# A transformer stack on one Trainium2 core: the modulation projection moves from TensorE to GpSimd

## The chip, the core and the metric

The program runs on one core of one Trainium2 chip. The metric is the device time of one execution in microseconds (us).

## What is computed

The program runs four layers on a sequence of 256 tokens of width 1024 (an attention branch, a residual with factor 8^0.25, a layer norm), and behind them one block with a modulated RMS norm, pooling and MoBA attention, and PEER experts (product keys, 16384 experts in two tables). The kinds of the four attention branches are MLA, sliding window (SWA), forgetting (Fox), MLA, with 16 heads each. All numbers are fp32.

The change concerns the modulation of the last block:

```python
def modulate(x, g, shift, scale):
    return rmsnorm(x, g) * (1 + scale[:, None, :]) + shift[:, None, :]

# w_ada: (1024, 6 * 1024), c: one condition vector of 1024
mod = silu(c) @ w_ada + b_ada      # 6 * 1024 numbers: shift, scale, gate, twice
```

It has one row of output. It depends on nothing that the layers compute, so it can be worked out at any time before the last block's norm.

## The kernel before

**The stream.** All large weights lie in one tensor, `stream`, as chunks of 1 MB (128 rows x 4 tiles x 512 columns) in the order of use. SP loads chunk after chunk into `raw` (2 slots, L411 to L415). A chunk is two pieces of two tiles. For each piece ScalarE writes a rounded high part into `w_hi` (L829), and VectorE the rest, raw minus high, into `w_lo` (L1058); these are rings of 4 pieces. TensorE multiplies high by high, high by low and low by high (`parts_product`, L504 to L506), so that three fp32r products give nearly fp32. Each piece is used once (`piece_used`), which frees its place in the ring. SP waits for `piece_lo` before it fills a slot again.

**The plan.** Every group of products whose sum is taken out of PSUM together is a `Unit` (L130), with its banks, its number of pieces and who takes it out how. Units alternate between two pairs of banks (0 to 3). `bank_free` (L488) waits for the unit before the last. Attention has banks 4 to 7: scores in 4 and 5, turned probabilities in 6, outputs in 7.

**A layer.** TensorE turns x (`xT`), projects it (q, k, v and gates; MLA in two steps with a norm and rotations between), does attention head by head, turns the outputs (`oT`) and projects them with the residual. VectorE's `layer_norm` (L1225) ends the layer. TensorE waits for it, half by half (`x_half`), before it turns x for the next layer.

**Attention** (L564 on TensorE, L873 on ScalarE, L1137 on VectorE). In step i TensorE does the scores of head i (L577; in Fox L581 too), one modulation piece (L552), the turn of head i-1's probabilities (L591) and the output of head i-2 (L601 to L603). VectorE scales and masks the scores (L1165, in SWA L1162), takes their negative maximum (L1169, L1170), and normalises an output by its row sum, times the gate (L1189). ScalarE takes the exponential (L889) and copies the turned probabilities back (L897). These three products are in fp32 without splitting.

**The modulation before.** Each layer has three units of 512 outputs, each of 4 pieces: 12 pieces in 12 of 16 steps (L569 on TensorE). The stationary operand is the condition's column, spread over 128 columns (`c_hi`, `c_lo`), so all 128 rows of the result are alike. ScalarE and VectorE split these pieces inside attention (L898, L1200), VectorE adds the bias to row 0 (L1116), and GpSimd stores the row in `mod_rows` in HBM and loads the next bias (L444 to L450). The weights stand in the stream between a layer's projections and its output weights (`lay_out`, L1572).

**GpSimd's queue before** holds DMA issues alone: start loads, stores and biases, gains of the layer norms (`ln_gb`, needs `ln_used`), and behind the last head (L460) the loads for MoBA: all six modulation rows spread over 128 partitions, gain, pool weights, bands.

**The silu of the condition** is on ScalarE in layer 0, in front of the building of k (L934). VectorE splits it behind the turns (L1312).

MoBA's attention (8 heads) uses the same `attention` with no modulation pieces.

Of the kernel before, what the change touches and what calls it, by code (L numbers as in the profile page):

```python
# [14 lines left out]
F32 = mybir.dt.float32  # L15
# [6 lines left out]
P = 128  # L22
S = 256
B = S // P
D = 1024
# [104 lines left out]
class Unit:  # L130
# [8 lines left out]
    def __init__(self, plan, kind, dst, how, ktiles=KD, cols=COLS, pieces=0, k0=0, col0=0, tiles=4, width=P, pair=None):  # L139
# [4 lines left out]
        self.pair = self.n % PAIRS if pair is None else pair  # L144
        last = plan[-1].count if plan else {"act": 0, "dve": 0}
# [19 lines left out]
def build(nc, x_in, stream, table_in, bands_in, ln_in, mla_norm_in, sinks_in, wf_in, bf_in, c_in, bada_in, g2_in,  # L165
          pool_w_in, pool_scale_in, aug_in, keys_in, x_spill, mod_rows, out):
    n_chunks = stream.shape[0]
    with ExitStack() as ctx:
# [16 lines left out]
        small = sb("small", [P, 64])  # L185

# [12 lines left out]
        c_hi = sb("c_hi", [P, KD], F32R)  # L199
        c_lo = sb("c_lo", [P, KD], F32R)  # L200
# [39 lines left out]
        mod_row = cut(26112, 2, COLS)  # L240
# [50 lines left out]
        def ada_units(l):  # L291

            return [Unit(plan, "own", [mod_row[0:1, n % 2]], [("dve", "add")], pieces=KD // PK)
                    for n in range(ADA_UNITS * l, ADA_UNITS * (l + 1))]

        layers = []
        for l in range(DEPTH):
# [3 lines left out]
            if kind == "mla":  # L301
# [6 lines left out]
                L["ada"] = ada_units(l)  # L308
                L["oT"] = split_turn_units(KD)
            elif kind == "swa":  # L310
# [3 lines left out]
                L["ada"] = ada_units(l)  # L314
                L["oT"] = split_turn_units(KD)
            else:
# [5 lines left out]
                L["ada"] = ada_units(l)  # L322
                L["oT"] = split_turn_units(KD)
            L["out"] = residual_units()
            layers.append(L)
# [45 lines left out]
        bada_loaded = [sem(f"bada_loaded{s}") for s in range(2)]  # L371
        c_silu, c_rep, h_ready, merged_ready = sem("c_silu"), sem("c_rep"), sem("h_ready"), sem("merged_ready")
# [25 lines left out]
        n_pieces = 2 * n_chunks  # L398
# [6 lines left out]
        def _(sp):  # L405
            sp.dma_start(x_tok, x_in.rearrange("(b p) d -> p b d", p=P)).then_inc(x_loaded, 16)
            sp.dma_start(kept[:, :], table_in[:, 0:KEPT_W]).then_inc(kept_loaded, 16)
            for s in range(RAW):
                sp.dma_start(raw[:, s], stream[s]).then_inc(chunk_landed[s], 16)
            sp.dma_start(arena[:, REST:REST + TABLE_W - KEPT_W], table_in[:, KEPT_W:]).then_inc(tables_loaded, 16)  # L410
            with sp.Fori(1, n_chunks // RAW) as turn:  # L411
                for s in range(RAW):

                    sp.wait_ge(piece_lo, 2 * RAW * turn - 2 * RAW + 2 * s + 2)
                    sp.dma_start(raw[:, s], stream[RAW * turn + s]).then_inc(chunk_landed[s], 16)  # L415
# [7 lines left out]
        def _(pool):  # L423
# [5 lines left out]

            load(c_col[:, :], c_in, c_loaded)  # L430
# [6 lines left out]
            def load_bias(n):  # L437
                load(mod_row[0:1, n % 2], bada_in[:, n * COLS:(n + 1) * COLS], bada_loaded[n % 2])

            for n in range(2):  # L440
                load_bias(n)
# [18 lines left out]
            pool.wait_ge(out_taken, DEPTH * HEADS)  # L460
            load(moba["mod"].rearrange("p a n -> p (a n)"), rows(mod_rows[0]), mod_loaded)
            load(gain, rows(g2_in[0]), g2_loaded)
            load(moba["pw"], pool_w_in, moba_loaded)
            load(moba["ps"], pool_scale_in, moba_loaded)

            pool.wait_ge(ln_used, DEPTH)
            load(moba["bands"].rearrange("p a b n -> p (a b n)"), bands_in, moba_loaded)

# [16 lines left out]
        def _(pe):  # L485
            piece = [0]

            def bank_free(unit):  # L488
                if unit.n >= PAIRS and unit.pair < PAIRS:
                    wait_put(pe, [plan[unit.n - PAIRS]])  # L490
# [61 lines left out]
            def ada_piece(units, i):  # L552

                u, first = units[i // (KD // PK)], i % (KD // PK) * PK
                if first == 0:
                    pe.wait_ge(c_rep, 1)
                    bank_free(u)
                w = take_piece()
                for k in range(first, first + PK):
                    mm = parts_product(bank_of(u, 0), [c[:, k:k + 1].broadcast_to([P, P]) for c in (c_hi, c_lo)],  # L560
                                       [x[:, k % PK] for x in w], k == 0, k == KD - 1)
                drop_piece(mm)

            def attention(heads, q, k, v, fox=False, ada=()):  # L564
# [54 lines left out]
            for L in layers:  # L619
# [7 lines left out]
                if L["kind"] == "mla":  # L627
# [12 lines left out]
                    for u in L["kT"]:  # L640
# [3 lines left out]
                              lambda h, b: mla["kv"][:, b, 2 * HD * h + HD:2 * HD * (h + 1)], ada=L["ada"])  # L644
                    o = mla["o"]
                elif L["kind"] == "swa":
# [4 lines left out]
                    def half(h):  # L651
# [5 lines left out]
                              lambda h, b: attn["v"][:, b, HD * (h // SWA_GROUP):HD * (h // SWA_GROUP + 1)], ada=L["ada"])  # L657
                    o = attn["o"]
                else:
# [10 lines left out]
                    for u in L["k"] + L["v"] + L["gate"]:  # L670
# [4 lines left out]
                              lambda h, b: attn["v"][:, b, HD * h:HD * (h + 1)], fox=True, ada=L["ada"])  # L675
# [139 lines left out]
        def _(act):  # L815
# [57 lines left out]
            def attention(heads, kind, ada=()):  # L873
                g0 = heads_done[0]
                before = ada[0].pieces_done - KD // PK if ada else 0
                for i in range(heads + 1):
# [21 lines left out]
                    if 1 <= i <= len(ada) * KD // PK:  # L898

                        split_ahead(before + i)  # L900
# [739 lines left out]
```

## Time and profile before

| | |
|---|---|
| median of 3 runs | 1908.87 us (1907.85 to 1910.93) |
| profiled execution, device time | 1908.54 us |
| its span | 1906.3 us |
| mean granted TensorE clock | 0.93 of full speed |
| TensorE busy | 1733.4 us, 91% |
| VectorE busy | 1285.2 us, 67% |
| ScalarE busy | 905.6 us, 48% |
| GpSimd busy | 23.8 us, 1% |
| HBM traffic | 283 MB, mean 148 GB/s |

Names in the profile: PE is TensorE's matmuls, PEld its weight loads, DVE VectorE, ACT ScalarE, POOL GpSimd. L504 is a line of the kernel above; a helper's line stands for all its callers. "Busy" of PE comes from modelled ends of pipelined products, so a busy PE isn't one at its peak. The granted clock is a share of 2.4 GHz: 0.50 is 1.2 GHz, and values between are the mean of a stretch that has both. Groups have the form: line, engine, operation, output<-inputs, shape, count | busy us, mean ns | idle time before them in us and who ended it. Most SBUF tensors are cuts of one tensor, `arena`.

### The profile page before, as it was taken

Reading aid. Unit: us, or ns where it says so; the run is one execution under the profiler, and the core shown is the slowest. Engines: PE = TensorE matmul, PEld = TensorE weight load, DVE = VectorE, ACT = ScalarE, POOL = GpSimd, SP = SyncE. Lnnn points to the kernel's source line nnn. Section 1 sums busy time; section 2 is a strip of 40 time slices with the busy share of each in tenths; the row PEclk is TensorE's granted clock in tenths of the full one; section 3 lists DMA queues with packets and bytes.
Section 4 is the critical chain, followed back from the end, with each engine's and each line's share of the span. In section 5 each row is a group of like instructions: output and inputs, shape, how many; then the busy total and the mean of one; then the engine's idle time right before and its main releaser. Section 6 shows DMA issues by size and latency. Waiting matters only on the chain.

```text
span 1906.3 us, 29464 instructions
## 1 busy us (share of the span) xinstructions
PE 1733.4 (91%) x10294; PEld 1534.0 (80%) x10294; DVE 1285.2 (67%) x2391; ACT 905.6 (48%) x1410; POOL 23.8 (1%) x50
## 2 busy tenths in 40 slices
PE   6788898898989787898879999899999999999996
PEld 5677787796867576686769999899999888888885
DVE  3666557544756685544555999777777888885554
ACT  4464355344543573343334666655555333334543
POOL 0000000000000000000000000000000000000000
PEclk8888897899988897896889999999999999999998
DMA  6423443355234434451343444433433343435552
GB/s 225 175 90 110 160 162 126 110 177 177 92 108 164 174 111 171 166 182 62 113 152 135 174 176 176 177 132 132 146 140 134 130 154 132 154 138 215 198 188 99
DMA packets 40323, 282.95 MB, mean 148 GB/s; under 512 B 5280, under 2 KB 5424, under 8 KB 6848
## 3 DMA queue, kind: packets, MB, share of 16 engines
q1 hardware_dynamic: 37136, 267.13, 39.7%
q0 software_dynamic: 3120, 14.94, 2.2%
q8 instruction: 40, 0.66, 0.1%
q14 instruction: 27, 0.22, 0.0%
HBM read 279.94 MB, written 2.12 MB: 148 GB/s over the span
## 4 chain that ended last, share of the span: by engine, by line
PE 73%; DVE 17%; ACT 4%; DMA 3%; issue 3%; DVEq 0%; SPq 0%; ACTq 0%
PE banks L504 20%; PE banks L506 19%; PE banks L505 19%; PE banks L771 6%; DVE w_lo L1058 5%; DMA raw<-stream 3%; PE banks L577 2%; PE banks L546 2%; PE banks L591 1%; ACT w_hi L829 1%; PE banks L603 1%; PE banks L602 1%; PE banks L601 1%; DVE arena L1440 1%; DVE arena L1247 1%
## 5 line engine op out<-in xcount | busy, mean ns | idle before, releaser
L1058 DVE TENSOR_TENSOR w_lo<-raw,w_hi 128x1024 fp32r<-128x1024 f32 x504 | 614.2, 1221 | 385.8 <-ACT w_hi L829 383.9
L829 ACT ACTIVATE w_hi<-raw 128x1024 fp32r<-128x1024 f32 x504 | 532.2, 1057 | 635.8 <-PE banks L506 549.1
L504 PE MATMUL banks<-w_hi,xT_hi 128*128 128x512 f32 (+2 forms) x1140 | 457.0, 401 | 25.9 <-DVE xT_lo L1090 15.4
L506 PE MATMUL banks<-w_hi,xT_lo 128*128 128x512 f32 (+2 forms) x1140 | 448.5, 393 | 0.0
L505 PE MATMUL banks<-w_lo,xT_hi 128*128 128x512 f32 (+2 forms) x1140 | 446.8, 392 | 0.0
L504 PE MATMUL banks<-xT_hi,w_hi 128*128 128x256 f32 x1360 | 394.8, 290 | 5.5 <-DVE w_lo L1058 2.6
L506 PE MATMUL banks<-xT_hi,w_lo 128*128 128x256 f32 x1360 | 388.8, 286 | 0.0
L505 PE MATMUL banks<-xT_lo,w_hi 128*128 128x256 f32 x1360 | 388.7, 286 | 0.0
L504 PEld LDWEIGHTS banks<-w_hi,xT_hi 128*128 128x128 f32 x1140 | 220.5, 193 | 72.7 <-issue 17.5
L504 PEld LDWEIGHTS banks<-xT_hi,w_hi 128*128 128x128 f32 x1360 | 265.0, 195 | 7.4 <-ACT arena L988 2.7
L505 PEld LDWEIGHTS banks<-xT_lo,w_hi 128*128 128x128 f32 x1360 | 264.7, 195 | 0.0
L506 PEld LDWEIGHTS banks<-xT_hi,w_lo 128*128 128x128 f32 x1360 | 264.3, 194 | 0.0
L506 PEld LDWEIGHTS banks<-w_hi,xT_lo 128*128 128x128 f32 x1140 | 219.1, 192 | 46.2
L505 PEld LDWEIGHTS banks<-w_lo,xT_hi 128*128 128x128 f32 x1140 | 220.7, 194 | 42.5
L546 PE MATMUL banks<-kept,arena 128*128 128x128 f32 (+1 forms) x354 | 69.8, 371 | 92.4 <-DVEq L1267 29.1
L546 PEld LDWEIGHTS banks<-kept,arena 128*128 128x128 f32 (+1 forms) x354 | 58.8, 189 | 101.5 <-DVEq L1267 30.8
L771 PEld LDWEIGHTS banks<-scratch 128*128 128x128 f32 x1024 | 129.9, 192 | 5.3
L771 PE MATMUL banks<-scratch 128*128 128x64 f32 x1024 | 128.2, 268 | 0.0
L889 ACT ACTIVATE scratch<-scratch,neg_max 128x128 f32<-128x128 f32 (+1 forms) x144 | 64.0, 445 | 75.1 <-DVE neg_max L1170 74.6
L1495 DVE TENSOR_TENSOR arena<-arena,banks 128x256 f32 (+1 forms) x128 | 53.7, 420 | 52.0 <-PE banks L771 52.0
L1485 DVE TENSOR_TENSOR scratch<-kept,scratch 128x512 f32<-128x512 f32 x128 | 87.6, 684 | 0.3 <-ACT scratch L869 0.3
L869 ACT ACTIVATE arena<-banks 128x512 f32<-128x512 f32 (+1 forms) x76 | 43.6, 587 | 85.0 <-PE banks L506 65.1
(178 smaller groups left out, 1589.8 us busy)
## 6 DMA issues: line engine op xcount, KB each, us to landing
raw<-stream SPq DMA_DIRECT2D x252, 1024.0 KB, 4.8
arena<-ln_in POOLq DMA_DIRECT2D x4, 1024.0 KB, 5.1
arena<-mod_rows POOLq DMA_DIRECT2D x1, 3072.0 KB, 10.1
arena<-g_in POOLq DMA_DIRECT2D x3, 512.0 KB, 9.6
arena<-x_in SPq DMA_DIRECT2D x1, 1024.0 KB, 5.1
arena<-bands_in POOLq DMA_DIRECT2D x1, 1024.0 KB, 5.2
arena<-keys_in POOLq DMA_DIRECT2D x1, 1024.0 KB, 5.2
x_spill<-arena POOLq DMA_DIRECT2D x1, 1024.0 KB, 5.0
```

The source lines that it names most:

```text
L504: pe.matmul(out, stationary[0], moving[0], start=first, stop=False, **k)
L505: pe.matmul(out, stationary[0], moving[1], start=False, stop=False, **k)
L506: return pe.matmul(out, stationary[1], moving[0], start=False, stop=last, **k)
L546: mm = pe.transpose(bank_of(unit, t // 2)[0:unit.width, (t % 2) * S + b * P:(t % 2) * S + (b + 1) * P], src[:, b, c:c + unit.width], ident)
L577: mm = pe.matmul(bank[:, cols[0]:cols[1]], qh[:, qb * P:(qb + 1) * P], kh[:, 0:n], start=(qb == 0), stop=not fox, skip_group_check=True)
L771: mm = pe.matmul(banks[:, 4 + s % 2, t * HALF:(t + 1) * HALF], hot2[:, s % 2, t], hot1[:, s % 2, t], start=(t == 0), stop=True, skip_group ...
L829: act.activation(w_hi[:, s], raw[:, s // 2, (s % 2) * PIECE:(s % 2 + 1) * PIECE], ACT.Copy).then_inc(piece_hi, 1)
L869: act.activation(dst, src, fn).then_inc(evac_act, 1)
L889: ins = act.activation(probs[:, g % 2, lo:hi], s_sb[:, g % 2, lo:hi], ACT.Exp, bias=neg_max[:, g % 4, b:b + 1], accum_out=row_sum[:, g % 4 ...
L1058: dve.tensor_tensor(w_lo[:, s], raw[:, s // 2, (s % 2) * PIECE:(s % 2 + 1) * PIECE], w_hi[:, s].bitcast(F32), ALU.subtract).then_inc(piece ...
L1485: dve.tensor_tensor(hot2[:, s % 2], keys.broadcast_to([P, GT, NKEYS]), picks[1].broadcast_to([P, GT, NKEYS]), ALU.is_equal)
L1495: dve.tensor_tensor(mine, mine, banks[:, 4 + s % 2, 0:GT * HALF].rearrange("p (t n) -> p n t", t=GT), ALU.mult).then_inc(g_taken, 1)
```

## The change

The modulation leaves the stream. GpSimd loads the weights tile by tile (128 rows x 512 columns, 256 KB), two slots (`ada_raw`), multiplies a tile by the condition's column (one number per partition) and adds it to one of three sums (`ada_sum`, 128 x 512), which start as zero with the bias in row 0. When a layer's 24 tiles are in, TensorE sums over the partitions: one product with ones per 512 outputs, in plain fp32, behind the layer's out projection, into banks 4 to 6. ScalarE copies row 0 of each back over the sum's row 0 and GpSimd stores it.

Attention has no modulation piece any more. SP's loop over the stream is written out for the layers, without their 24 modulation chunks (`n_pieces` is 456, not 504), and is a loop again behind them. The silu of the condition is ScalarE's first work. The modulation rows are loaded for the last block in two halves, the first behind layer 3's last head, the second when all are stored.

```diff
@@ plan
-        def ada_units(l):
-
-            return [Unit(plan, "own", [mod_row[0:1, n % 2]], [("dve", "add")], pieces=KD // PK)
-                    for n in range(ADA_UNITS * l, ADA_UNITS * (l + 1))]
+        def ada_units():
+
+            return [Unit(plan, "own", [t[0:1] for t in ada_sum[0:2]], [("act", "copy")] * 2, pair=2),
+                    Unit(plan, "own", [ada_sum[2][0:1]], [("act", "copy")], pair=3)]
...
             L["out"] = residual_units()
+            L["ada"] = ada_units()
@@ GpSimd
+            def load_tile(t):
+                k = t % CK
+                load(ada_raw[:, t % 2], stream[tile_chunk[t]][:, k * COLS:(k + 1) * COLS], tile_landed[t % 2])
...
+            for t in range(2):
+                load_tile(t)
+            pool.wait_ge(c_silu, 1)
             for l in range(DEPTH):
 
-                for i, u in enumerate(layers[l]["ada"]):
-                    n = ADA_UNITS * l + i
-                    wait_put(pool, [u])
-                    pool.dma_start(mod_rows[:, n * COLS:(n + 1) * COLS], mod_row[0:1, n % 2]).then_inc(mod_stored, 16)
-                    pool.wait_ge(mod_stored, 16 * (n + 1))
-                    if n + 2 < ADA_UNITS * DEPTH:
-                        load_bias(n + 2)
+                for i in range(ADA_UNITS):
+                    n = ADA_UNITS * l + i
+                    if l:
+                        pool.wait_ge(mod_stored, 16 * ADA_UNITS * l)
+                    pool.memset(ada_sum[i], 0.0).then_inc(sum_cleared, 1)
+                    pool.wait_ge(sum_cleared, n + 1)
+                    load(ada_sum[i][0:1], bada_in[:, n * COLS:(n + 1) * COLS], bada_loaded)
+                pool.wait_ge(bada_loaded, 16 * ADA_UNITS * (l + 1))
+                for i in range(ADA_UNITS):
+                    for k in range(KD):
+                        t = (ADA_UNITS * l + i) * KD + k
+                        pool.wait_ge(tile_landed[t % 2], 16 * (t // 2 + 1))
+                        pool.tensor_scalar(ada_raw[:, t % 2], ada_raw[:, t % 2], c_col[:, k:k + 1], None, ALU.mult).then_inc(tile_scaled, 1)
+                        pool.wait_ge(tile_scaled, t + 1)
+                        pool.tensor_tensor(ada_sum[i], ada_raw[:, t % 2], ada_sum[i], ALU.add).then_inc(ada_used, 1)
+                        pool.wait_ge(ada_used, t + 1)
+                        if t + 2 < DEPTH * ADA_UNITS * KD:
+                            load_tile(t + 2)
+                if l == DEPTH - 1:
+                    pool.wait_ge(out_taken, DEPTH * HEADS)
+                    load(moba["mod"][:, 0:3].rearrange("p a n -> p (a n)"), rows(mod_rows[0, 0:3 * D]), mod_loaded)
+                    load(gain, rows(g2_in[0]), g2_loaded)
...
+                for i in range(ADA_UNITS):
+                    n = ADA_UNITS * l + i
+                    wait_put(pool, [layers[l]["ada"][i // 2]])
+                    pool.dma_start(mod_rows[:, n * COLS:(n + 1) * COLS], ada_sum[i][0:1]).then_inc(mod_stored, 16)
@@ TensorE
-            def ada_piece(units, i):
...
+            def ada_rows(l):
+
+                pe.wait_ge(ada_used, ADA_UNITS * KD * (l + 1))
+                pe.wait_ge(out_taken, heads_done[0])
+                for i in range(ADA_UNITS):
+                    mm = pe.matmul(banks[:, 4 + i], const("ones")[:, 0:P], ada_sum[i], start=True, stop=True)
+                    if i:
+                        mm.then_inc(unit_full, 1)
...
                 for i in range(heads + 2):
                     if i < heads:
                         scores(i)
-                    if i < len(ada) * KD // PK:
-                        ada_piece(ada, i)
...
                 for i, u in enumerate(L["out"]):
                     project(u, L["oT"][1:] if i == 0 else ())
+                ada_rows(l)
@@ ScalarE
-                    if 1 <= i <= len(ada) * KD // PK:
-
-                        split_ahead(before + i)
...
             act.wait_ge(eps_ready, 1)
+            act.wait_ge(c_loaded, 16)
+            act.activation(c_col[:, :], c_col[:, :], ACT.Silu).then_inc(c_silu, 1)
...
                 deviation(root, 1.0, 4, mean_var[:, :, 1])
+                for u in L["ada"]:
+                    evacuate_only(u)
@@ VectorE
-                    if 2 <= i <= len(ada) * KD // PK + 1:
-                        split_ahead(before + i - 1)
-                        if (i - 1) % (KD // PK) == 0:
-                            evacuate_only(ada[(i - 1) // (KD // PK) - 1])
```

## Rows read from the trace of the kernel before

**Rows 1.** Page, parts head and 2: span, and clock granted in 40 slices.
```profile
span 1906.3 us, 29464 instructions
...
PEclk8888897899988897896889999999999999999998
```

**Rows 2.** Page, part 4: the chain that ended last, by line.
```profile
PE banks L504 20%; PE banks L506 19%; PE banks L505 19%; PE banks L771 6%; DVE w_lo L1058 5%; DMA raw<-stream 3%; PE banks L577 2%; PE banks L546 2%; PE banks L591 1%; ACT w_hi L829 1%; PE banks L603 1%; PE banks L602 1%; PE banks L601 1%; DVE arena L1440 1%; DVE arena L1247 1%
```

**Rows 3.** Groups by line and form, TensorE: one of three modulation groups.
```profile
L504 PE MATMUL banks<-w_hi,c_hi 128*128 128x512 f32 x96 | 45.3, 472 | 0.0
```

**Rows 4.** Busy by window, four attentions; last columns clock, DMA share, GB/s.
```profile
118.26:161.45 43.19, 39.71 (x249) 34.03 (x248) 38.84 (x99) 31.78 (x85) 2.42 (x5) 1.00 0.38 128
271.65:321.33 49.68, 46.02 (x243) 35.75 (x242) 44.22 (x128) 34.27 (x102) 2.44 (x5) 0.92 0.42 143
474.09:533.92 59.83, 58.62 (x313) 46.76 (x314) 43.71 (x113) 31.38 (x86) 2.44 (x5) 0.93 0.31 106
673.16:717.24 44.08, 40.08 (x243) 34.08 (x242) 38.88 (x99) 32.80 (x87) 1.96 (x4) 0.95 0.39 135
```

**Rows 5.** Busy by window, layer attention without modulation pieces beside it.
```profile
471.00:477.00 6.00, 5.85 (x15) 4.00 (x16) 1.78 (x6) 0.98 (x4) 0.00 (x0) 0.50 0.27 112
529.40:541.00 11.60, 10.05 (x41) 8.60 (x39) 4.75 (x18) 3.21 (x11) 0.97 (x2) 0.50 0.26 91
713.20:725.00 11.80, 9.11 (x38) 7.97 (x39) 5.77 (x20) 3.63 (x13) 0.48 (x1) 0.50 0.26 91
```

**Rows 6.** Busy by window, MoBA attention: six steps, then one step.
```profile
882.01:903.58 21.57, 20.42 (x73) 15.60 (x74) 9.74 (x35) 9.13 (x34) 0.00 (x0) 0.50 0.00 1
889.26:892.84 3.58, 3.58 (x14) 2.81 (x15) 1.72 (x7) 1.36 (x5) 0.00 (x0) 0.50 0.00 0
```

**Rows 7.** Timeline, layer 0 attention: start us, us, engine line, [idle before].
```profile
119.65 0.56 DVE L1165 SCALAR_TENSOR_TENSOR scratch<-banks,arena 128x384 f32<-128x384 f32 x1 [0.18 <-PE banks L577]
...
161.45 0.55 DVE L1165 SCALAR_TENSOR_TENSOR scratch<-banks,arena 128x384 f32<-128x384 f32 x1
...
164.18 0.87 PE L591 MATMUL banks<-kept,scratch 128*128 128x128 f32 x3 [0.55 <-ACT scratch L897]
```

**Rows 8.** Timeline, TensorE: ends of attention in layers 3 and 2.
```profile
708.10 0.52 PE L591 MATMUL banks<-kept,scratch 128*128 128x128 f32 x3 [0.98 <-ACT scratch L897]
...
709.08 0.87 PE L577 MATMUL banks<-arena 96*128 96x128 f32 x4
...
713.77 0.88 PE L591 MATMUL banks<-kept,scratch 128*128 128x128 f32 x3 [0.99 <-ACT scratch L897]
...
717.18 0.87 PE L591 MATMUL banks<-kept,scratch 128*128 128x128 f32 x3
...
528.99 0.87 PE L591 MATMUL banks<-kept,scratch 128*128 128x128 f32 x3 [0.44 <-ACT scratch L897]
...
533.82 0.90 PE L591 MATMUL banks<-kept,scratch 128*128 128x128 f32 x3
```

**Rows 9.** Groups by line and form, VectorE: two inputs in SBUF.
```profile
L1265 DVE TENSOR_TENSOR arena<-arena 128x512 f32<-128x512 f32 x8 | 5.2, 687 | 0.1
```

**Rows 10.** DMA issues: a load of 256 KB by GpSimd, us to landing.
```profile
arena<-aug_in POOLq DMA_DIRECT2D x1, 256.0 KB, 5.7
```

**Rows 11.** Timeline, GpSimd, when layer 0 ends.
```profile
207.14 0.56 POOL L425 DMA_DIRECT2D arena<-ln_in  x1 [42.08 <-DVEq L1252]
```

**Rows 12.** Timeline, TensorE: last product of layer 1.
```profile
357.21 0.39 PE L506 MATMUL banks<-w_hi,xT_lo 128*128 128x512 f32 x1
```

**Rows 13.** Groups by line and form, VectorE, 207 to 271 us.
```profile
L1058 DVE TENSOR_TENSOR w_lo<-raw,w_hi 128x1024 fp32r<-128x1024 f32 x21 | 25.7, 1225 | 32.9 <-ACT w_hi L829 32.7
```

**Rows 14.** Start: busy by window, and ScalarE's timeline.
```profile
10.00:16.00 6.00, 0.39 (x3) 0.15 (x2) 1.60 (x2) 3.55 (x4) 0.00 (x0) 0.79 1.01 402
...
15.73 1.06 ACT L829 ACTIVATE w_hi<-raw 128x1024 fp32r<-128x1024 f32 x1 [0.42 <-DMA raw<-stream]
```

**Rows 15.** Timeline, TensorE, layer norm of layer 0.
```profile
203.76 1.97 PE L546 MATMUL banks<-kept,arena 128*128 128x128 f32 x8 [6.52 <-DVEq L1250]
```

More of the change, by code:

```diff
@@ L144, in __init__ @@
         self.pair = self.n % PAIRS if pair is None else pair
+        same = [u for u in plan if u.pair == self.pair]
+        self.before = same[-1] if same else None
         last = plan[-1].count if plan else {"act": 0, "dve": 0}
@@ L321, in build @@
                 L["gate"] = token_units(attn["gate"], D, SILU2)
-                L["ada"] = ada_units(l)
                 L["oT"] = split_turn_units(KD)
+            L["chunks"] = (plan[-1].pieces_done - (layers[-1]["out"][-1].pieces_done if layers else 0)) // 2
             L["out"] = residual_units()
+            L["ada"] = ada_units()
             layers.append(L)
@@ L407, in _ @@
             sp.dma_start(kept[:, :], table_in[:, 0:KEPT_W]).then_inc(kept_loaded, 16)
[L408 to L411, printed above, removed]
+            landed, at = 0, 0
+            for L in layers:
+                n_in, n_out = L["chunks"], 2 * D // COLS
+                for n in list(range(at, at + n_in)) + list(range(at + n_in + ADA_CHUNKS, at + n_in + ADA_CHUNKS + n_out)):
+                    if landed >= RAW:
+                        sp.wait_ge(piece_lo, 2 * (landed - RAW) + 2)
+                    sp.dma_start(raw[:, landed % RAW], stream[n]).then_inc(chunk_landed[landed % RAW], 16)
+                    landed += 1
+                    if landed == RAW:
+                        sp.dma_start(arena[:, REST:REST + TABLE_W - KEPT_W], table_in[:, KEPT_W:]).then_inc(tables_loaded, 16)
+                at += n_in + ADA_CHUNKS + n_out
+            with sp.Fori(at // RAW, n_chunks // RAW) as turn:
                 for s in range(RAW):
-                    sp.wait_ge(piece_lo, 2 * RAW * turn - 2 * RAW + 2 * s + 2)
+                    sp.wait_ge(piece_lo, 2 * RAW * turn - 2 * RAW + 2 * s + 2 - 2 * DEPTH * ADA_CHUNKS)
                     sp.dma_start(raw[:, s], stream[RAW * turn + s]).then_inc(chunk_landed[s], 16)
@@ L428, in rows @@
                 return src.partition_broadcast(P)
+            tile_chunk, at = [], 0
+            for L in layers:
+                at += L["chunks"]
+                tile_chunk += [at + n // CK for n in range(ADA_UNITS * KD)]
+                at += ADA_CHUNKS + 2 * D // COLS
+            def load_tile(t):
+                k = t % CK
+                load(ada_raw[:, t % 2], stream[tile_chunk[t]][:, k * COLS:(k + 1) * COLS], tile_landed[t % 2])
             load(c_col[:, :], c_in, c_loaded)
@@ L458, in _ @@
                     load(mla["g"], rows(mla_norm_in[1]), norm_loaded)
[L460 to L464, printed above, removed]
             pool.wait_ge(ln_used, DEPTH)
             load(moba["bands"].rearrange("p a b n -> p (a b n)"), bands_in, moba_loaded)
+            pool.wait_ge(mod_stored, 16 * DEPTH * ADA_UNITS)
+            load(moba["mod"][:, 3:6].rearrange("p a n -> p (a n)"), rows(mod_rows[0, 3 * D:]), mod_loaded)
             pool.wait_ge(h_ready, 1)
@@ L488, in bank_free @@
             def bank_free(unit):
-                if unit.n >= PAIRS and unit.pair < PAIRS:
-                    wait_put(pe, [plan[unit.n - PAIRS]])
+                if unit.before is not None and unit.pair < PAIRS:
+                    wait_put(pe, [unit.before])
             def take_piece():
@@ L550, in _, with attention @@
             heads_done = [0]
-            def ada_piece(units, i):
[L554 to L564, printed above, removed]
+            def ada_rows(l):
[5 more added lines that the diff above has]
+                        mm.then_inc(unit_full, 1)
+            def attention(heads, q, k, v, fox=False):
                 g0 = heads_done[0]
@@ L871, in _, with attention @@
             heads_done = [0]
-            def attention(heads, kind, ada=()):
+            def attention(heads, kind):
                 g0 = heads_done[0]
-                before = ada[0].pieces_done - KD // PK if ada else 0
                 for i in range(heads + 1):
@@ L1133, in _, with attention @@
             heads_done = [0]
-            biases = [0]
             gated = s_sb[:, :, :].rearrange("p a n -> p (a n)")[:, 0:COLS].unsqueeze(1)
-            def attention(heads, kind, scale, o, gate, ada=()):
+            def attention(heads, kind, scale, o, gate):
                 g0 = heads_done[0]
-                before = ada[0].pieces_done - KD // PK if ada else 0
                 def head_rows(h):
@@ L1323, in _ @@
                     wait_put(dve, L["gate"])
-                    attention(HEADS, "swa", HD ** -0.5, attn["o"], attn["gate"], L["ada"])
+                    attention(HEADS, "swa", HD ** -0.5, attn["o"], attn["gate"])
                 else:
@@ L1346, in _ @@
                     settle()
-                    attention(HEADS, "fox", HD ** -0.5, attn["o"], attn["gate"], L["ada"])
+                    attention(HEADS, "fox", HD ** -0.5, attn["o"], attn["gate"])
                 for u in L["oT"]:
```

43 lines of the change are left out of this document (16 added, 27 removed).

## The prediction

> **What bounds the kernel now.** I read the page first. The profiled execution lasts 1906.3 us inside a run of 1908.54 us (2.2 us lie around the span), and that run is 0.3 us below the median of the three runs, 1908.87; every sum below starts from 1908.54. The tenths of the granted clock in the page's second part are mostly 8 and 9 in the first half and 9 behind it [rows 1]: TensorE doesn't always have its full clock. The fourth part, the chain that ended last, is mostly TensorE, and of that mostly projections [rows 2]. GpSimd computes nothing, so it is free.
>
> The 48 modulation pieces (288 products: the group shown and two like it [rows 3]) all stand in the first 12 of 16 heads of the four layers' attention. So the change has to be read in four stretches. I cut them from the first to the last score pass of VectorE (L1165 or L1162), 15 steps from head to head: 43.19, 49.68, 59.83 and 44.08 us, together 196.8 us [rows 4]. The granted clock is 1.00 (2.4 GHz) over the first one and 0.92 to 0.95 over the others, and the reader is to see why: where the pieces have ended it is 0.50 (1.2 GHz) [rows 5]. The fifth attention of the kernel, MoBA's, has no such pieces. There the clock is 0.50 from end to end, with TensorE occupied for 20.4 of 21.6 us, and a head takes 3.58 us [rows 6]. It is a picture of what attention looks like when modulation has left it.
>
> **Part 1: the pieces leave the heads.** Gone are 12 times 6 products per layer on TensorE, 12 splits each on ScalarE and VectorE, and three adds on VectorE. What a head costs without them depends on the clock.
>
> At 2.4 GHz: from VectorE's score pass (161.45) to the turn of the probabilities on TensorE (164.18) are 2.73 us [rows 7]; from the start of a turn (708.10) through the head's outputs to the end of the next scores (709.08 + 0.87) are 1.85 us [rows 8]. Scores run one head ahead, so this loop of 2.73 + 1.85 + 0.1 serves two heads: 2.34 us a head. It is less than the 2.9 us of today (43.19 / 15), so work does leave the path, since today VectorE's split of 1.22 us stands in each head.
>
> At 1.2 GHz: an MLA head goes from turn to turn in 717.18 - 713.77 = 3.41 us with no wait in front [rows 8], a MoBA head in 3.58 us [rows 6], and a forgetting head, which has two more products, in 533.82 - 528.99 = 4.83 us [rows 8]. TensorE then is the bound by its own slowness, and ScalarE and VectorE, now relieved, only wait.
>
> I take 1.2 GHz, because every attention of the trace shows it as soon as nothing but head work is left: in both tails of [rows 5], and in MoBA [rows 6], where TensorE never waits and yet the clock doesn't rise. The products with the modulation weights are dense 512-column work that fills the gaps between heads, so they hold the clock; the change removes just these. The Trainium skill says the same as a rule (TensorE: Matmul & The Clock Gate, "The HAM clock gate"): the slow clock is the default and only activity releases it. By it this change costs; by TensorE's removed work alone it would gain; the trace agrees with the rule.
>
> Stretch by stretch, with a few steps at full clock after a warm projection:
> - MLA, layers 0 and 3: the first step as now, 1.4 (118.26 to 119.65 [rows 4, 7]), one of 2.3, then 13 of 3.41: 48.0 us against 43.19 and 44.08: +4.8 and +3.9.
> - Sliding window: 1.4, two of 2.6 (2.34 and the sink's small operations), 12 of 3.58: 49.6 against 49.68: -0.1.
> - Forgetting: its attention begins cold already (0.50 from 471 to 477 [rows 5]), so a first step of 2.9, one of 3.5 (no outputs yet) and 13 of 4.83: 69.2 against 59.83: +9.4.
>
> Sum of part 1: +18.0 us. What follows attention starts at 1.2 GHz before and after, so it doesn't change. If the clock holds one step longer in each stretch, that takes off 1.1 us in each.
>
> **Part 2: GpSimd's work.** Per layer it issues three clears, three bias loads and 24 tiles: a load of 256 KB, a product, a sum. No row shows GpSimd computing. The nearest is VectorE's 128x512 with both inputs in SBUF, 0.69 us [rows 9]; for lack of a nearer row I bound one operation by 0.69 and by three times that. A load of that size took 5.7 us to land [rows 10], and an issue takes 0.56 us of GpSimd [rows 11]. With two buffers a tile takes the larger of its own work (two operations and an issue, 1.9 to 4.7 us) and half of load plus own work (3.8 to 5.2 us): 3.8 to 5.2 us, 91 to 125 us a layer. The sliding layer leaves least time, from 207.1 us [rows 11] to the end of its out projection at 357.6 us [rows 12], 6.0 us a tile after the bias loads. So it is hidden. A page only prices the sum: the Trainium skill (GPSIMD Engine Reference, "Elementwise") has 4.5 us for 2048 elements, an estimate of 1.1 us for 512.
>
> Queued behind the 24 tiles on GpSimd's queue are the stores of the modulation rows, the next norm's gains (needed a whole layer later) and, in layer 3, the loads for MoBA, which even before could only start behind the last head. None is late at that pace.
>
> **Contention.** The splits before attention read two SBUF tensors, and VectorE sat idle 32.9 us in front of 21 of them, 1.6 us each [rows 13]; a delay by a GpSimd operation goes into that. On the path are only some norm and rotation operations. Bounds 0 (all in idle time) and 66 us (each of 96 tiles delays the path once by 0.69 us); I take 2 us, near the lower end, since splits have that cover.
>
> **Part 3: start.** From 10 to 16 us the DMA engines are full, 402 GB/s, and ScalarE waits for the second chunk until 15.73 us [rows 14]. Two tiles more, 0.5 MB, at that rate: +1.3 us (0 if they come last). The silu of the condition moves from the path of layer 0 to the start, but its table is then loaded in front of the gates' silu: nothing.
>
> **Part 4: ada_rows.** TensorE waits for the last tile, then does three fp32 products of 512 columns behind the out projection. A head's scores, 384 columns in fp32, take 0.87 us at full clock [rows 8], so three times 512 columns cost 3.5 us (7 at half the clock, but the projection leaves it full), and TensorE is idle there for 6.52 us for the layer norm [rows 15]. ScalarE's three copies of a row lie in front of its first evacuation. Nothing; if that cover went, up to 3.5 us a layer. SP's loads in attention vanish (24 chunks), and nobody waited for them.
>
> **Sum:** 1908.5 + 18.0 + 2 + 1.3 = 1929.8, say 1930 us.
>
> **The rivals.**
> 1. **The clock stays at 2.4 GHz** (the other side). For it: the heads then come closer together than in today's tails, where VectorE still splits. Stretches: 34.2 twice, 36.4 with the sink's operations, and for the forgetting heads 15 of 2.65 (half of 4.83 - 3.58 at full clock, over two heads), 39.8: 144.6 against 196.8, so 1908.5 - 52.2 + 3.3 = 1860 us. Against it: four tails and MoBA. It decides from about a third of the way: the cold sum is 214.8, and 193.5 breaks even.
> 2. **Only the forgetting layer gets the full clock**, since its heads have the most TensorE work: 2.9 + 3.5 + 13 times 2.65 = 40.9 against 59.83, -19, so 1908.5 + 8.6 - 19 + 3.3 = 1901 us. For it: no row shows a longer run of such heads without pieces. Against: its own tail fell to 0.50 too [rows 5].
> 3. **VectorE is held up by GpSimd.** If GpSimd's operations push VectorE's back wherever both run, a third of the 66 us above may reach the path in place of 2: 1950 us. For it: both read SBUF at once in the projections; against: the idle time of [rows 13]. The Trainium skill (SBUF — State Buffer, "Who interferes with whom") says that a VectorE instruction with two SBUF inputs and a GpSimd instruction that reads SBUF exclude each other; no row of before, where GpSimd doesn't compute, can show it.
> 4. **GpSimd is late**, and TensorE waits in ada_rows. It decides at 6.0 us a tile in the sliding layer and at 7.0 in layer 3; at 8 us it is 48 + 24 us more, 2002 us. Against: the upper bound is 5.2.
>
> **Chances.** Forecast 0.66 (own range 1920 to 1942); rivals 0.08, 0.14, 0.08, 0.04. About 0.2% (3.8 us) is what a measurement of this kernel can tell. Faster by more: rival 1 and most of rival 2, 0.19; within: the rest of it, 0.07; slower 0.74. The range goes from 1899 (rival 2) to 1945 us.
>
> **What would show it.** In the changed profile: granted clock 0.50 over most of each attention and MLA heads 3.4 us apart, forgetting heads 4.8; VectorE and ScalarE less busy there; a GpSimd that finishes its 24 tiles before the heads end; three products in the idle time of the layer norm. Heads of 2.3 us at clock 1.00 would prove me wrong, and so would TensorE waiting for GpSimd's sums, or VectorE's splits clearly above 1.22 us and on the chain.

## The result, and the profile after

The changed kernel takes 1938.0 us (median of 4 runs, 1936.1 to 1947.2) against 1908.5 us before, measured beside it. The ratio is 1.0162, 95% interval 1.0127 to 1.0196: slower by 29.5 us. Forecast were 1930 us and a range from 1899 to 1945.

The profiled execution lasts 1936.13 us, its span is 1934.3 us. First the page after: span, busy time by engine, granted clock.

```profile
span 1934.3 us, 28816 instructions
PE 1749.2 (90%) x10030; PEld 1541.6 (80%) x10030; DVE 1271.8 (66%) x2329; ACT 865.4 (45%) x1374; POOL 398.9 (21%) x351
...
PEclk8776885899558788897779999999999999999998
```

TensorE has 264 products fewer and is busy 16 us longer. GpSimd is at work for 399 us (24 before). The clock has new dips where attention is ([rows 1] has none at 5).

Next the four layer attentions by window, cut as in [rows 4], from first to last score pass. Columns: stretch, length, busy time (and instructions) of PE, PEld, DVE, ACT and POOL, clock, DMA share, GB/s.

```profile
124.68:170.82 46.14, 43.82 (x178) 39.18 (x179) 24.58 (x85) 21.29 (x75) 2.98 (x3) 0.52 0.04 12
279.43:333.72 54.29, 49.45 (x177) 38.11 (x178) 37.64 (x113) 22.80 (x89) 41.13 (x36) 0.51 0.25 83
488.65:557.91 69.26, 67.96 (x236) 53.64 (x235) 28.82 (x99) 20.00 (x74) 3.15 (x3) 0.50 0.03 8
711.34:746.04 34.70, 26.74 (x176) 21.59 (x176) 24.58 (x85) 21.12 (x75) 1.53 (x2) 0.91 0.00 1
```

Three of four are at about 1.2 GHz (0.50 to 0.52) and longer than before, by 3.0, 4.6 and 9.4 us. The fourth, layer 3's, is at 0.91 and 9.4 us shorter. Together they take 204.4 us against 196.8: +7.6 us. I call everything else in the span "the rest": 1934.3 - 204.4 = 1729.9 us, against 1709.5 before, +20.4 us. So most of the loss lies outside attention, in stretches whose TensorE work the change doesn't touch. The worst are those from the latent norm to the end of q's rotation in the two MLA layers. Here they are after, layers 0 and 3:

```profile
50.34:101.04 50.70, 37.95 (x158) 31.50 (x156) 37.06 (x50) 20.49 (x26) 44.66 (x35) 0.78 0.60 213
635.36:687.33 51.97, 38.29 (x164) 31.48 (x162) 37.39 (x49) 20.71 (x26) 46.82 (x38) 0.80 0.62 221
```

And before, the same two stretches:

```profile
49.51:91.83 42.32, 33.09 (x158) 26.81 (x156) 27.98 (x50) 20.73 (x26) 0.00 (x0) 0.88 0.52 182
608.57:649.78 41.21, 32.74 (x164) 26.96 (x162) 28.07 (x49) 20.84 (x26) 0.00 (x0) 0.92 0.54 199
```

+8.4 and +10.8 us, with the same 50 and 49 instructions on VectorE, which are busy 9 us longer. (TensorE's clock is lower there too. That it isn't the cause shows below: e8 has 0.80 in layer 0's stretch and takes 42.95 us.) The timeline of VectorE and GpSimd in layer 3's rotation shows why (start us, us, engine line):

```profile
680.06 1.38 POOL L477 TENSOR_TENSOR arena<-arena 128x512 f32<-128x512 f32 x1
680.20 1.52 DVE L1227 TENSOR_TENSOR arena<-arena 128x256 f32<-128x256 f32 x1
681.64 0.41 DVE L1228 TENSOR_TENSOR arena<-arena 128x256 f32<-128x256 f32 x1
...
684.24 1.26 POOL L477 TENSOR_TENSOR ada_spare<-arena,ada_spare 128x512 f32<-128x512 f32 x1
684.26 1.51 DVE L1228 TENSOR_TENSOR arena<-arena 128x256 f32<-128x256 f32 x1
```

An operation of 0.41 us that starts during GpSimd's sum lasts 1.5 us: it ends 0.28 us after GpSimd's does. GpSimd's own groups over the whole span (the third sum lies in `ada_spare`):

```profile
L475 POOL TENSOR_SCALAR arena<-arena,c_col 128x512 f32<-128x512 f32 x96 | 172.9, 1801 | 33.1 <-DMA ada_spare<-bada_in 25.5 <-DMA arena<-stream 3.6
L477 POOL TENSOR_TENSOR arena<-arena 128x512 f32<-128x512 f32 x64 | 96.2, 1503 | 5.3
L477 POOL TENSOR_TENSOR ada_spare<-arena,ada_spare 128x512 f32<-128x512 f32 x32 | 42.3, 1320 | 2.7
```

GpSimd's operations are stretched as well: the shortest product took 1.56 us and the shortest sum 1.26 us, where the means are 1.80 and 1.50.

### The profile page after: what moved, and what is told of

It reads as the page before. It is cut to its first block, busy times and chain, and to the rows that moved or that the text cites. A ratio compares the mean times of both kernels' runs of the same rounds, so it can differ in the third digit from the quotient of the medians.

```text
span 1934.3 us, 28816 instructions
## 1 busy us (share of the span) xinstructions
PE 1749.2 (90%) x10030; PEld 1541.6 (80%) x10030; DVE 1271.8 (66%) x2329; ACT 865.4 (45%) x1374; POOL 398.9 (21%) x351
## 4 chain that ended last, share of the span: by engine, by line
PE 71%; DVE 16%; ACT 5%; DMA 4%; issue 3%; DVEq 0%; SPq 0%; ACTq 0%
PE banks L541 18%; PE banks L543 17%; PE banks L542 17%; PE banks L804 6%; DMA raw<-stream 4%; DVE w_lo L1088 4%; PE banks L611 4%; PE banks L625 2%; PE banks L583 2%; ACT w_hi L862 1%; PE banks L637 1%; PE banks L636 1%; PE banks L615 1%; PE banks L635 1%; ACT scratch L921 1%
## 5 line engine op out<-in xcount | busy, mean ns | idle before, releaser
L1088 DVE TENSOR_TENSOR w_lo<-raw,w_hi 128x1024 fp32r<-128x1024 f32 x456 | 577.4, 1269 | 378.9 <-ACT w_hi L862 376.9
L862 ACT ACTIVATE w_hi<-raw 128x1024 fp32r<-128x1024 f32 x456 | 482.0, 1058 | 663.0 <-PE banks L543 532.1
L543 PEld LDWEIGHTS banks<-w_hi,xT_lo 128*128 128x128 f32 x1140 | 223.1, 196 | 46.8
L475 POOL TENSOR_SCALAR arena<-arena,c_col 128x512 f32<-128x512 f32 x96 | 172.9, 1801 | 33.1 <-DMA ada_spare<-bada_in 25.5
L611 PE MATMUL banks<-arena 64*128 64x128 f32 (+3 forms) x288 | 103.1, 502 | 12.7 <-DVE arena L1170 10.2
```

The costliest lines, as they stand in the source:

```text
L475: pool.tensor_scalar(ada_raw[:, t % 2], ada_raw[:, t % 2], c_col[:, k:k + 1], None, ALU.mult).then_inc(tile_scaled, 1)
L543: return pe.matmul(out, stationary[1], moving[0], start=False, stop=last, **k)
L611: mm = pe.matmul(bank[:, cols[0]:cols[1]], qh[:, qb * P:(qb + 1) * P], kh[:, 0:n], start=(qb == 0), stop=not fox, skip_group_check=True)
L862: act.activation(w_hi[:, s], raw[:, s // 2, (s % 2) * PIECE:(s % 2 + 1) * PIECE], ACT.Copy).then_inc(piece_hi, 1)
L1088: dve.tensor_tensor(w_lo[:, s], raw[:, s // 2, (s % 2) * PIECE:(s % 2 + 1) * PIECE], w_hi[:, s].bitcast(F32), ALU.subtract).then_inc(piece ...
```

## The experiments

Stretches are cut in each profile as above. "Attentions" is the sum of the four layers' windows, "rest" is the span less that. The ratio is taken over the executions of a run, and isn't quite the quotient of two medians. "Hold n" stands for n added products a step in the sliding window, forgetting and MoBA attentions; MLA attention has two in e4, e5, e6 and e9, and four in e7.

| | median us | ratio to before | span | attentions | rest |
|---|---|---|---|---|---|
| before | 1908.5 | | 1906.3 | 196.8 | 1709.5 |
| changed | 1938.0 | 1.0162 | 1934.3 | 204.4 | 1729.9 |
| e1 no tiles | 1923.5 | 1.0071 | 1906.9 | 201.9 | 1705.0 |
| e2 loads, writes only | 1922.5 | unclear | 1914.1 | 202.5 | 1711.6 |
| e3 products and sums only | 1935.6 | 1.0168 | 1922.2 | 203.0 | 1719.2 |
| e4 hold 2 | 1957.8 | 1.0250 | 1954.5 | 220.0 | 1734.5 |
| e5 hold 4 | 1894.1 | 0.9916 | 1896.7 | 176.4 | 1720.3 |
| e6 hold 6 | 1908.3 | 1.0003 | 1910.2 | 181.8 | 1728.4 |
| e7 before, hold 4 | 1888.6 | 0.9898 | 1883.3 | 193.9 | 1689.4 |
| e8 pause | 1935.4 | 1.0135 | 1934.9 | 214.2 | 1720.7 |
| e9 hold 4 and pause | 1879.3 | 0.9840 | 1882.6 | 175.2 | 1707.4 |

e2's four times scatter too far for a ratio (1895.9 to 2254.9 us); only its profile is used.

Span, attentions and rest are those of one profiled execution, which can lie far from the median: e1's took 1908.7 us (median 1923.5), e3's 1924.1 us (median 1935.6, the others 1935.0 to 1950.5). How much one stretch varies can be read off before the first score pass, up to which the changed kernel, e4, e5 and e6 have the same program: they reach it at 124.7, 127.6, 128.4 and 124.8 us; the kernel before and e7 at 118.3 and 115.2. A difference of 3 to 4 us in one stretch of one profile shows nothing by itself.

### Which part of GpSimd's work costs: e1, e2, e3

e1:

```diff
-            for t in range(2):
-                load_tile(t)
...
-                for i in range(ADA_UNITS):
-                    for k in range(KD):
...
-                pe.wait_ge(ada_used, ADA_UNITS * KD * (l + 1))
+                pe.wait_ge(bada_loaded, 16 * ADA_UNITS * (l + 1))
```

> Edit: the changed kernel without its 96 tile loads, products and sums (left out: the product with the modulation weights; the sums hold only the bias). Everything else, ada_rows too, stays. In the changed kernel's profile the four layer attentions together take 204.4 us (196.8 before) and all the rest is 20.4 us longer than before. Theory: attention is slow by the clock alone and the rest by GpSimd's work, so here the rest falls back to the 1709.5 us of before (within 3) while attention stays at 1.2 GHz, about 200 to 218 us: time about 1912 to 1930 us. Rival (the rest comes from the order of the stream or from ada_rows): the rest stays 15 us or more above before and the time near 1936.

e2, in place of product and sum (TensorE waits for the biases here too):

```diff
+                        for j in range(6):
+                            pool.memset(ada_raw[:, t % 2], 0.0).then_inc(ada_used, 1)
+                            pool.wait_ge(ada_used, 6 * t + j + 1)
```

> Edit: the changed kernel with all 96 tile loads, but in place of product and sum six clears of the tile per tile, so that GpSimd is about as busy and loads at about the same pace, yet only writes SBUF (left out: the product with the modulation weights). If GpSimd's reads hold VectorE: VectorE's two-input operations keep 1.22 us per split, and the time is that of the kernel without tiles plus at most 4 us for the loads. If the loads (or GpSimd's activity as such) cost the 20 us: the time stays within 5 us of the changed kernel.

e3 drops `load_tile` and the waits for it:

> Edit: the changed kernel with products and sums over two tiles cleared once, and no tile loads (left out: the real weights). If GpSimd's reads hold VectorE: most of the 20 us outside attention stays (15 us or more over the kernel without tiles). If the loads do it: within 4 us of the kernel without tiles.

Without tiles the rest is 1705.0 us, 4.5 less than before (forecast was within 3): no cost of ada_rows or of the new order of the stream is to be seen. The operations of VectorE, in layer 3's projections, with writes only (e2):

```profile
L1087 DVE TENSOR_TENSOR w_lo<-raw,w_hi 128x1024 fp32r<-128x1024 f32 x27 | 32.8, 1223 | 28.1 <-ACT w_hi L861 27.7
L1230 DVE TENSOR_TENSOR arena<-arena 128x256 f32<-128x256 f32 x2 | 0.8, 424 | 0.1
```

and with products and sums but no loads (e3; the second line is the same operation of the rotation, and of its six the one that was held most):

```profile
L1085 DVE TENSOR_TENSOR w_lo<-raw,w_hi 128x1024 fp32r<-128x1024 f32 x27 | 39.2, 1465 | 26.9 <-ACT w_hi L859 26.6
L1228 DVE TENSOR_TENSOR arena<-arena 128x256 f32<-128x256 f32 x2 | 2.9, 1448 | 0.1
```

In e2 GpSimd is busy for about as long (387 us) and loads all tiles, and these two-input operations of VectorE keep their times of before (1.22 and 0.42 us). In e3 it loads nothing, and they are stretched as in the changed kernel, whose splits take 1.45 us there. VectorE's 2329 instructions are busy for 1227.1 us in e1, 1231.7 in e2, 1263.9 in e3 and 1271.8 in the changed kernel. And the two stretches from the latent norm to the rotation show it directly. With writes only (e2):

```profile
50.30:93.93 43.63, 33.02 (x158) 26.77 (x156) 27.96 (x50) 20.50 (x26) 36.10 (x69) 0.88 0.66 238
626.75:667.83 41.08, 32.84 (x164) 27.05 (x162) 28.03 (x50) 20.85 (x26) 35.12 (x68) 0.92 0.70 256
```

and with products and sums but no loads (e3):

```profile
49.11:100.42 51.31, 37.46 (x158) 31.46 (x156) 39.38 (x50) 20.73 (x26) 48.85 (x28) 0.81 0.43 152
624.73:675.37 50.64, 38.38 (x164) 32.00 (x162) 38.23 (x49) 20.84 (x26) 48.09 (x29) 0.82 0.45 163
```

e1 has 40.6 and 41.6 us for them, about as long as before. So VectorE's operations with two inputs in SBUF are held up by GpSimd instructions that read SBUF, not by GpSimd being busy with writes, and not by its DMA. That is what the Trainium skill states (SBUF — State Buffer, "Who interferes with whom").

In the rest, e3 stands 14.2 us over e1, just under the 15 expected. e2 stands 6.6 us over e1, more than the 4 expected, but it is 5.9 us later at the first score pass, 3.3 us longer in the stretch behind it and 4.0 us shorter behind layer 2's attention, so whether loads cost anything isn't shown. Both together (the changed kernel) stand at +24.9.

e1 shows a second thing, the two MLA attentions, layers 0 and 3:

```profile
114.03:148.76 34.73, 26.77 (x176) 21.61 (x176) 24.56 (x85) 21.14 (x75) 0.00 (x0) 0.91 0.00 1
672.79:718.93 46.14, 43.82 (x178) 39.19 (x179) 24.55 (x85) 21.32 (x75) 0.00 (x0) 0.50 0.00 1
```

Same code, same kernel: one at full clock, one at half, 11.4 us apart, and the other way round than in the changed kernel. An MLA attention without pieces can go either way. e1's ten times fall into two groups: three lie at 1908.4 to 1909.2, seven at 1922.4 to 1928.6. The profiled execution is of the lower group and has one slow MLA attention; a second one would add 11.4 us, and the groups are 13 to 20 apart, so this may be part of the difference but not all of it, and no slower execution has a trace. The changed kernel's spread (1936 to 1947) would fit it too, and isn't shown either. Forgetting attention took 69.3 us and was at 0.50 in every changed kernel without added products.

### Is it the clock: e4, e5, e6, e7

These add products that nobody reads, behind each step's scores, with n per step (`hold`). The edit has one thing more, which isn't printed here: in front of the heads TensorE waits for the next piece's split, and behind the first scores for the gate's sums to be taken out of PSUM (sliding window and forgetting), since the added products read the one and write over the other.

```diff
+                    if i < heads + 1:
+                        for _ in range(hold):
+                            pe.matmul(banks[:, 0], w_hi[:, piece[0] % RING, 0:P], w_hi[:, piece[0] % RING, 0:COLS], start=True, stop=True)
```

> Edit: the changed kernel with two idle-time products (128 x 512, fp32r, w_hi by w_hi into bank 0, whose result nobody reads) in each step of all five attentions, behind the scores. Clock theory: if these 0.47 us a step keep 2.4 GHz, MLA heads come 2.4 to 2.6 us apart, forgetting heads 2.7 to 3.1, MoBA heads 2.4 to 2.6, the five attentions take 160 to 185 us in place of 227, and the time falls by 40 to 60 us below the changed kernel, to 1875 to 1900, below the kernel before. If two are too few: clock 0.5 and each cold step 0.85 us longer, 1990 us. Rival (heads are slow for another reason than the clock, the chain through ScalarE and VectorE): the steps grow or stay as they are, whatever the clock.

> Edit: the changed kernel with idle-time products as in e4, two a step in MLA attention, but four in the sliding window, forgetting and MoBA attentions. With two a step these three stayed at 0.50 (64.3, 84.3, 28.8 us). Clock theory: what counts is how dense the work is; if four are enough the clock is above 0.9 there and TensorE's own steps are 1.85 + 0.94 = 2.8 us, forgetting 3.4: 42 to 44, 51 to 53 and 20 to 21 us, time 1895 to 1910. If four are still too few, each cold step grows by another 0.85 us: 77, 97, 35 us and 1985 us. Rival (the clock has nothing to do with the extra products): clock 0.50 whatever their number.

> Edit: as e5, with six a step in the sliding window, forgetting and MoBA attentions, which is the product count of a modulation piece. Clock theory: clock above 0.9 there as in the kernel before, steps of about 3.27 us (forgetting 3.9), so 49, 58 and 23 us, and the time 1912 to 1925: the 20 us that GpSimd's work costs outside attention stay. Rival: the clock stays at 0.50 and the time goes above 2000 us.

e7 has them in the kernel before the change, in steps without a modulation piece:

> Edit: the kernel before the change, its modulation pieces in place, with four idle-time products in each step that has no piece: the last steps of the four layer attentions and all of MoBA's. Clock theory: MoBA's 22.7 us fall to about 20 and the tails gain 1 to 3 us each, with the turns and the first products behind them at full clock: 5 to 20 us faster than before, 1888 to 1903, and faster than both kernels. If the clock isn't held: 10 to 25 us slower.

Sliding window, forgetting and MoBA attention with two products a step (e4):

```profile
272.31:336.65 64.34, 61.54 (x203) 46.67 (x203) 33.92 (x114) 22.81 (x89) 37.71 (x33) 0.51 0.19 66
491.74:576.05 84.31, 84.31 (x271) 65.03 (x271) 29.35 (x98) 20.02 (x74) 4.09 (x4) 0.50 0.02 7
922.17:950.97 28.80, 28.80 (x91) 20.87 (x91) 10.93 (x37) 9.14 (x34) 0.00 (x0) 0.50 0.00 1
```

and with four (e5):

```profile
274.23:319.93 45.70, 43.83 (x233) 33.56 (x234) 34.19 (x114) 22.80 (x90) 36.19 (x32) 0.93 0.26 87
470.88:528.91 58.03, 58.03 (x301) 45.57 (x302) 29.14 (x99) 20.24 (x74) 10.02 (x9) 0.89 0.06 19
876.59:898.44 21.85, 21.85 (x105) 16.10 (x106) 10.94 (x37) 9.25 (x34) 0.00 (x0) 0.85 0.00 0
```

With twice as many added products these attentions take 18.6, 26.3 and 7.0 us less. TensorE has more to do, and nothing was taken from ScalarE or VectorE; what fell is the time of TensorE's own products, with the clock at 0.85 to 0.93 in place of 0.5. So the clock theory stands and the rival (the chain through ScalarE and VectorE) falls. e4's own forecast failed: two products were too few for these three, and its 1957.8 us lie between the 1875 to 1900 of one case and the 1990 of the other, since MLA attention did hold its clock. e5's time (1894.1) lies just below its 1895 to 1910, but its attentions are longer than forecast, 58.0 us for forgetting where 51 to 53 stood: a step took 3.57 us, not 3.4, and the first three took 4.9, 5.5 and 4.8. MLA attention, 35.0 to 36.4 us, was at 0.91 to 0.95 in all of e4, e5, e6 and e9, eight times of eight. With six products, as many as a modulation piece had, the clock is 1.00 and 0.97 in sliding window and forgetting attention, 48.4 and 60.7 us, 2.7 and 2.6 us more than with four. In all, e6 is as fast as the kernel before: 1.0003 (0.9987 to 1.0020), a little under its 1912 to 1925, and its rest of 1728.4 us still has what GpSimd costs. That it comes out even is no measure of what the change lost by the clock, since the products speed up stretches that were at 0.50 before the change as well, as e7 shows.

e7 is within its forecast, 0.9898 (0.9879 to 0.9916). Its four attentions gain only 2.9 us, MoBA's 1.0. Of the 20 us by which the rest is shorter, 16 lie behind the five attentions, where work follows a tail that now ends at full clock. Here are the 4.0 us of layer 0, from its last score pass to the turning of x, in e7 and in the kernel before:

```profile
158.32:196.66 38.34, 28.33 (x142) 23.15 (x140) 22.11 (x39) 14.88 (x24) 0.49 (x1) 0.96 0.30 105
161.45:203.76 42.31, 32.25 (x137) 26.85 (x137) 22.19 (x39) 14.98 (x24) 0.48 (x1) 0.81 0.26 95
```

The other 3.1 us lie before the first score pass, where e7 changes nothing.

### Keeping GpSimd off the path: e8, e9

```diff
+                        if l % 3 == 0 and KD * i + k == 7:
+                            pool.wait_ge(q_roped, l // 3 + 1)
```

> Edit: the changed kernel, but in the two MLA layers GpSimd does seven tiles and then waits until the rotation of q has ended before the other 17. In the changed kernel the stretch from the latent norm to the end of the rotation lasts 50.7 us (layer 0) and 52.0 us (layer 3), against 42.3 and 41.2 before. Theory (GpSimd's reads hold VectorE on the path there): the stretch falls back to 41 to 44 us in both layers, the time by 12 to 19 us, to 1919 to 1928, give or take the 11.4 us by which one MLA attention differs between its two clocks. Rival (the delay comes from elsewhere): the stretch stays near 50 us, the time within 5 us of the changed kernel. If GpSimd then ends too late, TensorE waits in ada_rows and the rest grows instead.

> Edit: e5 (four idle-time products a step, two in MLA) with the pause of e8. If the two costs are independent they add: e5's 1894.1 less 12 to 19 us, 1875 to 1882 us, below the 1888.6 of the kernel before with idle-time products. If holding the clock had already hidden GpSimd's interference, the pause gives less than 5 us more.

The two norm-to-rotation stretches with the pause (e8):

```profile
50.74:93.69 42.95, 36.31 (x158) 30.30 (x156) 29.50 (x50) 20.72 (x26) 4.16 (x4) 0.80 0.54 194
628.90:674.76 45.86, 37.69 (x164) 31.47 (x162) 32.61 (x49) 20.84 (x26) 9.37 (x8) 0.81 0.54 197
```

Layer 0's falls from 50.7 to 43.0 us, as forecast. Layer 3's falls from 52.0 to 45.9, two short of it: there GpSimd still does eight operations in the stretch (POOL, 9.37 us). The rest is 9.2 us shorter than in the changed kernel. The time missed its forecast, 1935.4 us where 1919 to 1928 stood. In the profile both MLA attentions are at 0.50 (46.14 us each), where the changed kernel had one at 0.91: 11.4 us lost by that, near the 9.2 won. The forecast had named this difference; that e8's three other executions had it too isn't shown. With the clock held, where no such chance is left, the pause shows its worth: e9's two stretches take 43.1 and 46.8 us (e5 52.2 and 50.2), and e9 takes 1879.3 us, 14.8 less than e5, within its forecast. At 0.9840 (0.9823 to 0.9856) it is faster than both kernels and than e7.

## Why the prediction was right in direction, and where its sum was off

**The loop and the slow heads** were right in size. The prediction had 3.41 us for a slow MLA head, 3.58 for a sliding one, 4.83 for a forgetting one, 2.34 at full clock. VectorE's score passes are 3.20 us apart in layer 0, 3.58 to 3.86 in layer 1, 4.86 in layer 2, and alternate between 2.2 and 2.4 in layer 3. Forgetting attention was forecast to the digit (69.2, measured 69.26), partly by luck: its first two steps took 1.4 and 4.7 us where 2.9 and 3.5 stood. MLA in layer 0 came to 46.14 for a forecast of 48.0. The row that I took 3.41 from (the turn at 717.18 in [rows 8]) wasn't free of pieces. VectorE still had the last split and the bias add in front of that head's score pass, and the turn follows such a pass by 2.7 us, as in [rows 7]; a step without them takes 3.20. VectorE in the kernel before:

```profile
712.73 1.22 DVE L1058 TENSOR_TENSOR w_lo<-raw,w_hi 128x1024 fp32r<-128x1024 f32 x1
713.86 0.67 DVE L1116 TENSOR_TENSOR arena<-banks,arena 1x512 f32<-1x512 f32 x1
714.46 0.53 DVE L1165 SCALAR_TENSOR_TENSOR scratch<-banks,arena 128x384 f32<-128x384 f32 x1
```

**The sliding window** came to 54.3 for a forecast of 49.6. The two steps at full clock that the forecast had weren't there (e1, without tiles: 3.87 and 3.58 us for them, 51.8 in all), and GpSimd adds the rest. From its seventh score pass (299.26) to the last but one (330.14) every step takes 3.86 us. VectorE's sink operation, two numbers a row and 0.23 us by itself, is held as well, as the timeline of VectorE and GpSimd in the changed kernel shows:

```profile
308.02 1.27 POOL L477 TENSOR_TENSOR ada_spare<-arena,ada_spare 128x512 f32<-128x512 f32 x1
308.22 1.10 DVE L1196 TENSOR_SCALAR neg_max<-neg_max,neg_sink 128x2 f32<-128x2 f32 x1
```

This operation is held by clears too, which only write. In e2 it took up to 0.90 us, and here 0.54, beside three clears in a row:

```profile
285.80 1.69 POOL L476 MEMSET arena<- 128x512 f32 x3
286.39 0.54 DVE L1195 TENSOR_SCALAR neg_max<-neg_max,neg_sink 128x2 f32<-128x2 f32 x1
```

So what e2 shows of writes holds for the two-input operations, not for every operation of VectorE.

**Layer 3's attention** is the term of part 1 that failed. "I take 1.2 GHz" was wrong for it in this execution; rival 1 was right there, and with 34.70 us its price (34.2) was too. The forecast took one clock for all four, and no rival had the two MLA layers differ. e1 shows that for MLA it is open, and the difference is 11.4 us each. Part 1 was forecast at +18.0 and is +7.6 in this profile.

**Contention** is the other term. I took 2 us "near the lower end, since splits have that cover". The cover argument holds where it was made, in the long projections of layers 1 and 2: the stretch up to layer 1's attention is 1.6 us shorter than before, that up to layer 2's 2.2 us longer, neither more than a stretch varies by itself. Yet the splits did come out longer, one of the signs that the prediction had named against itself: 1.45 us in layer 3's projections, not 1.22. The argument doesn't hold in MLA's norm, short projections and rotation, where two-input operations of VectorE follow one another on the path: +8.4 and +10.8 us. These two stretches are 19.2 us of the rest's +20.4. Rival 3, with 22 us for contention in place of 2, describes them. So the forecast's 1930 was near 1938 partly because two errors of opposite sign met: 10 us too much for attention, 17 too little beside it.

**GpSimd's pace** was right: 4.2 to 4.4 us a tile in a layer's mean (forecast 3.8 to 5.2), and its tiles landed in 3.2 us (bounded by 5.7). An operation took 1.3 to 1.8 us in the mean of its group, twice to nearly three times VectorE's 0.69; TensorE never waited for its sums. Rival 4 is out.

**ada_rows** is hidden, as said, and cheaper than the 3.5 us estimated. In layer 0 it runs from 204.62 to 207.36, before x is turned:

```profile
204.62 1.88 PE L594 MATMUL banks<-arena 128*128 128x512 f32 x4
...
206.34 1.02 PE L594 MATMUL banks<-ada_spare,arena 128*128 128x512 f32 x2
...
211.28 1.23 PE L583 MATMUL banks<-kept,arena 128*128 128x128 f32 x8 [3.93 <-DVEq L1269]
```

**The start** is 0.9 us later (first projection at 20.46 us, before at 19.54) for 1.3 forecast.

**Left open:** whether the loads cost anything in the rest (+6.6 us in e2). At the start of layer 0's rotation e2 is 3.3 us behind e1 (89.87 and 86.57 us, 0.3 us of it from the start), but over layer 3's stretch it is 0.5 us faster than e1. The rest also varies with the clock in the projections: between rotation and first head, layer 0 took 26.4 us in the profile before (clock 0.74) and 23.6 us in the changed one (0.89). What decides which clock an MLA attention gets, no run shows.

## What to carry to other kernels

Work that fills an engine's waiting time may be paying for something: here the modulation products held TensorE's clock through attention, and to remove them cost more than they did. Before moving elementwise work to GpSimd, look for VectorE operations on the path that read SBUF twice while it would run, and put GpSimd's share elsewhere. Where the profile shows 0.50 in a stretch that TensorE bounds, a few idle products are a quick trial. Their number matters: four a step in the three attentions made both kernels faster, two made the changed one slower (1957.8 us), since these attentions stayed at 0.50 and had more to do.

## What the runs showed that I had not expected

- The clock of one piece of code is not fixed: MLA attention without added products was at 0.50 or at 0.91 to 0.95, about 46.1 or 34.7 us, within one execution even.
- TensorE can be at work without a gap and still have half its clock: with two added products a step, forgetting attention kept TensorE's records busy for 84.31 of 84.31 us and stayed at 0.50; with four it rose to 0.89.
- Loops on two engines can lock to one another: eight sliding-window steps in a row took 3.86 us, as GpSimd's tiles beside them did, and not their own 3.58.
